# A hybrid decoder step on one core: gate-up weights by halves, dealt parts, idle products and an earlier pick

## The reference

```python
h = rms_norm(x, g_mix); z = h @ w_in              # 1024 -> 4096
... # pooling mixer, gated convolution, two merge gates, w_o
x = x + mixed @ w_o

xt = rms_norm(x, g_ffn)                            # 264 rows count
logits = xt @ w_router + b_router                  # 32 experts
top_val, top_idx = lax.top_k(logits, 4); gates = softmax(top_val)
# for each expert e, over the rows that picked it:
hgu = x_e @ w_gu[e] + b_gu[e]                      # 1024 -> 2048, 8 MiB of weights
gate = minimum(hgu[:, :1024], 7); up = clip(hgu[:, 1024:], -7, 7)
y_e = (gate * sigmoid(1.702 * gate) * (up + 1)) @ w_down[e] + b_down[e]   # 4 MiB
x = x + sum over the four experts of gate * y_e
y = rms_norm(x, g_final)
```

## Time and profile before

| | |
|---|---|
| median of 3 runs | 1090.71 us (1090.71 to 1091.31) |
| the profiled execution | 1091.32 us |
| its span | 1089.5 us |
| busy: PE, PEld, DVE, ACT, POOL | 1049.2, 510.2, 462.5, 174.2, 8.9 us |
| packets of DMA, bytes | 52479, 432.63 MB, mean 397 GB/s |
| granted clock of TensorE | 0.997 of full speed |

### The profile page before, as it was taken

How to read it: one execution, slowest core, us unless ns; L and a number is a source line. 1 busy time by engine, 2 the same in 40 slices (tenths; PEclk the granted TensorE clock), 3 DMA queues, 4 the chain that set the end, 5 groups by cost and what they waited for, 6 DMA issues and landing times.

```text
span 1089.5 us, 17315 instructions
## 1 busy us (share of the span) xinstructions
PE 1049.2 (96%) x7081; PEld 510.2 (47%) x7081; DVE 462.5 (42%) x780; ACT 174.2 (16%) x296; POOL 8.9 (1%) x21
## 2 busy tenths in 40 slices
PE   8999999999999999999999999999999999999995
PEld 7999975434433444434344333333444333333332
DVE  5577675333333333333333333333333333333344
ACT  5435533100000000000000000000000000000012
POOL 1000100000000000000000000000000000000000
PEclk9999999999999999999999999999999999999998
DMA  9872899999999999999999999999999999999994
GB/s 295 289 227 103 324 405 375 429 420 426 428 429 427 429 428 430 427 429 428 429 428 428 429 428 428 428 429 428 428 429 428 429 428 429 429 428 431 426 425 170
DMA packets 52479, 432.63 MB, mean 397 GB/s; under 512 B 4630, under 2 KB 21546, under 8 KB 26205
## 3 DMA queue, kind: packets, MB, share of 16 engines
q1 hardware_dynamic: 50959, 431.04, 95.3%
q10 hardware_dynamic: 1494, 1.22, 0.4%
HBM read 431.10 MB, written 1.39 MB: 397 GB/s over the span
## 4 chain that ended last, share of the span: by engine, by line
PE 65%; DMA 26%; DVE 4%; issue 4%; ACT 1%; SPq 1%; DVEq 0%; ACTq 0%
PE PS L1153 24%; PE PS L1182 17%; DMA down_ring<-in_w_down_dram 14%; DMA gu_ring<-in_w_gu_dram 11%; PE PS L918 9%; PE PS L1082 3%; PE PS L1122 2%; PE PS L949 2%; PE PS L1124 1%; PE PS L1196 1%; PE PS L1166 1%; PE PS L1164 1%; DVE pick_twice L1596 1%; PE PS L1200 1%; PE PS L869 0%
## 5 line engine op out<-in xcount | busy, mean ns | idle before, releaser
L1153 PE MATMUL PS<-gu_ring,XgT 128*64 128x512 f32 x2048 | 470.5, 599 | 6.7 <-DMA gu_ring<-in_w_gu_dram 6.7
L1153 PEld LDWEIGHTS PS<-gu_ring,XgT 128*64 128x64 f32 x2048 | 134.5, 136 | 272.0 <-issue 244.5
L1182 PE MATMUL PS<-down_ring,actT 128*64 128x512 f32 x984 | 219.3, 596 | 7.7 <-DMA down_ring<-in_w_down_dram 7.7
L1628 DVE TENSOR_TENSOR Y<-PS,Y 128x1024 f32<-128x1024 f32 (+1 forms) x96 | 117.0, 1220 | 253.7 <-PE PS L1124 253.7
L1182 PEld LDWEIGHTS PS<-down_ring,actT 128*64 128x64 f32 x984 | 67.5, 137 | 134.8 <-issue 119.3
L1666 DVE SCALAR_TENSOR_TENSOR y_low<-PS,slot_gate,y_high 128x512 fp32r<-128x512 f32 x31 | 23.3, 750 | 228.6 <-ACT y_high L804 228.6
L816 ACT ACTIVATE work<-PS 128x512 f32<-128x512 f32 x32 | 19.1, 597 | 454.8 <-PE PS L1153 454.8
L918 PE MATMUL PS<-h_high,win_high 128*128 128x264 f32 (+2 forms) x256 | 71.2, 287 | 0.0
L918 PE MATMUL PS<-h_high,win_low 128*128 128x264 f32 (+2 forms) x256 | 70.9, 286 | 0.0
L918 PE MATMUL PS<-h_low,win_high 128*128 128x264 f32 (+2 forms) x256 | 70.8, 285 | 0.0
L804 ACT ACTIVATE y_high<-PS,slot_gate 128x512 fp32r<-128x512 f32 x31 | 21.3, 687 | 258.9 <-PE PS L1182 258.9
(11 more groups left out here) (236 smaller groups left out, 778.2 us busy)
## 6 DMA issues: line engine op xcount, KB each, us to landing
gu_ring<-in_w_gu_dram SPq DMA_DIRECT2D x119, 2048.0 KB, 28.5
down_ring<-in_w_down_dram SPq DMA_DIRECT2D x60, 2048.0 KB, 21.2
gu_ring<-in_w_gu_dram SPq DMA_DIRECT2D x18, 1024.0 KB, 10.0
gu_ring<-in_w_in_dram SPq DMA_DIRECT2D x16, 1024.0 KB, 9.4
gu_ring<-in_w_down_dram SPq DMA_DIRECT2D x4, 1024.0 KB, 28.3
down_ring<-in_w_down_dram SPq DMA_DIRECT2D x3, 1024.0 KB, 9.4
down_ring<-in_w_pool_up_dram SPq DMA_DIRECT2D x1, 2048.0 KB, 11.6
gu_ring<-in_w_conv_out_dram SPq DMA_DIRECT2D x2, 1024.0 KB, 6.2
```

Source lines behind the costliest of these rows:

```text
L1153: last = mm(PS[SLOTS * h:SLOTS * h + SLOTS, b, :], XgT[:, k, :], w[:, D * b + HALF * h:D * b + HALF * h + HALF], start=(k == 0), stop=(k = ...
L1182: last = mm(PS[SLOTS * h:SLOTS * h + SLOTS, bank, :], acts[:, f % 4, f // 4, :], rows[:, f, HALF * h:HALF * h + HALF], start=(f == 0), sto ...
L1628: tt(Y[rows, t, :].rearrange("p (h n) -> p h n", h=2), PS[rows, bank:bank + 2, :], Y[rows, t, :].rearrange("p (h n) -> p h n", h=2), ALU.a ...
```

## The change

**Halves.** For items 4 to 29 and the second half of item 3, `load_half` loads 4 MiB at once: four k-steps, a partition reads four adjacent rows, a run of 32 KB. SP waits for four k-steps to be free, not two; PE waits before k-steps 0 and 4 only. Items 2, 3 (first half), 30 and 31 are still loaded by row or chunk, with semaphores of their own. The chunks now lie inside the halves' layout: a run of 16 KB out of every 32. The step between features that are dealt to one partition is four in place of two, everywhere.

**Dealt parts.** `part` and `keep_rest` read `Y` with a step of four and write the parts in the order in which the gather takes them, so its weights (`XP`) are contiguous.

**Idle products.** `fill_early` puts a product of 512 columns of ones at three places of the routing chain.

**Picks.** In `item` on DVE, `make_twice` stands ahead of `add_rows`.

```diff
-                by_r = gffn_rows.rearrange("m (p r) -> m r p", r=2)
-                for q in range(2):
+                by_r = gffn_rows.rearrange("m (p r) -> m r p", r=CH)
+                for q in range(CH):
...
+            def load_half(e, parity, h):
+                src = w_gu[0, bass.ds(e, 1), HALF * h:HALF * h + HALF, :].rearrange("a (p r) n -> (a p) (r n)", r=CH)
+                at = KT * parity + CH * h
+                sp.dma_start(gu_ring[:, at:at + CH, :].rearrange("p s n -> p (s n)"), src
+                             ).then_inc(half_landed[2 * parity + h], 16)
...
-            def item_gu(i, e, parity, chunks=range(CH)):
-                for m in chunks:
-                    sp.wait_ge(gu_used, 8 * i + (2 * m - 14))
-                    load_gu(e, parity, m)
+            def item_gu(i, e, parity, halves=range(2)):
+                for h in halves:
+                    sp.wait_ge(gu_used, 8 * i + (4 * h - 12))
+                    load_half(e, parity, h)
+
+            def item_chunk(i, e, parity, m, signal):
+                sp.wait_ge(gu_used, 8 * i + (2 * m - 14))
+                load_gu(e, parity, m, signal)
...
-            item_gu(2, 2, 0, (1, 2, 3))
-            item_gu(3, 3, 1)
+            for m, signal in ((1, half_landed[0]), (2, third_chunk), (3, half_landed[1])):
+                item_chunk(2, 2, 0, m, signal)
+            for m, signal in ((0, fourth_chunk), (1, half_landed[2])):
+                item_chunk(3, 3, 1, m, signal)
+            item_gu(3, 3, 1, (1,))
...
+            for u in range(2):
+                for m in range(CH):
+                    item_chunk(more * E + (E - 2 + u), E - 2 + u, u, m, gu_landed[CH * u + m])
+                item_down(more * E + (E - 3 + u), E - 3 + u)
...
-                nc.scalar.activation(dst, Y[rows, t, cols], ACT.Copy, scale=stat[rows, 3, t:t + 1]
+                nc.scalar.activation(by_fours(dst), dealt(Y[rows, t, cols]), ACT.Copy, scale=stat[rows, 3, t:t + 1]
...
             pe.wait_ge(pick_early, 1)
+            fill_early()
             pe.wait_ge(resid, 5)
             turn_rows(1, 1)
             turn_tails()
+            fill_early()
             pe.wait_ge(x2_kept, 5)
...
-                stt(rests[(t, h)][rows, :], Y[rows, t, cols], stat[rows, 3, t:t + 1], src, ALU.mult, ALU.subtract
-                    ).then_inc(first_rest, 1)
+                stt(by_fours(rests[(t, h)][rows, :]), dealt(Y[rows, t, cols]), stat[rows, 3, t:t + 1], by_fours(src),
+                    ALU.mult, ALU.subtract).then_inc(first_rest, 1)
...
                 if before is not None:
                     swiglu(before, e_before)
+                    make_twice(before)
                 if two_before is not None:
                     for t in range(NT):
                         add_rows(two_before, t)
-                if before is not None:
-                    make_twice(before)
```

## The result

The changed kernel takes 1095.84 us (median of 5 runs, 1094.54 to 1097.69) beside 1090.72 us before (5 runs, 1090.71 to 1092.03): a ratio of 1.0046, 95% interval 1.0033 to 1.0059. Run once more, in a later group, it gave 1.0047 (1.0034 to 1.0060). So it is slower by about 5 us. The profiled execution has a span of 1093.3 us (1095.14 with what lies around it), 3.8 us over the 1089.5 us before. In the new code the gate-up product is L1193 (before L1153), the down product L1222 (L1182), ACT's first parts L761 (L732), DVE's rests L1516 (L1477), the first gather from `Y` L1136 (L1101), the load of a half L440.

The account below looks back on a forecast made before the run. It took the DMA queue, never empty from about 190 us on, as the bound; +1.5 - 1.5 + 0 + 0.1 - 0.2 + 0.1 = 0.0 us left the median at 1090.7 us, range 1087.2 to 1094.6.

Parts of the forecast that it names:

- both costs together: Queue running dry before item 4 at 4.2 us plus costlier strided ACT and DVE reads: 1095.6 us, left outside the range.
- the gap: Queue of transfers before item 4's first half, requested at 227.60 us, 4.24 us later than before: +1.5 us, bound 4.2.
- Part 3: Twelve ACT and DVE instructions reading `Y` at 16 bytes, six in series before the first gate-up: 0, between 0 and +2.2 us.
- The case: Rival: the six strided ACT and DVE reads in series cost 0.37 us more each: 1092.9 us, chance 0.15.
- part 4: Three idle PE products in the routing chain, mostly within waits, win nothing as the clock is full: +0.1 us.
- Part 1: Halves in place of chunks: item 4's first request comes 4.24 us later, the queue runs dry: +1.5 us, between 0.5 and 4.2.
- the full price of 4.2 us: Rival: the queue runs dry for most engines from 223.4 to 227.6 us: 1093.4 us, slower, chance 0.2.
- no later half could starve the queue: After item 4, PE returns slots every 27.6 us, the queue takes 29.4, so the stock grows 1.8 us per item.
- The tail's last wait is the same: At the end, items 30 and 31 keep 2 MiB chunks, so the last wait for a load doesn't change.
- Part 2: Gate-up loads in runs of 32 KB move faster over 53 halves, 519 us of queue: -1.5 us, between 0 and -3.6.
- the row of 425 GB/s: Single-row loads in 8 KB runs, 167 to 175 us, moved 425 GB/s; possibly a little low, so the gain too large.
- Part 5: Picks made right behind the SwiGLU end PE's 0.3 us wait per item; only the last, in the tail, counts: -0.2 us.

Follow-up runs that it names:

- early_two: The changed kernel with everything up to item 1 back at a step of two and the parts in plain order: 1089.78 us, 0.9986 of the kernel before.
- chunk_four: `early_two` with the first half of item 4 loaded as two 2 MiB chunks: 1090.45 us, 0.9986 of the kernel before.
- both_ends: `late_halves` with items 28 and 29 loaded by chunks too: 1090.01 us, 0.9989 of the kernel before.
- picks_only: The kernel before with only the picks of the way back made ahead of the additions: 1090.57 us, 0.9989 of the kernel before.
- all_chunks: `early_two` with every gate-up load as four 2 MiB chunks in the new layout: 1091.59 us, 1.0002 of the kernel before.
- reads_only: The changed kernel with every gate-up load as 2 MiB chunks, strided reads kept: 1098.46 us, 1.0065 of the kernel before.
- no_idle: The changed kernel without the three idle products of the routing chain: 1095.69 us, 1.0037 of the kernel before.
- late_halves: `early_two` with items 2 to 7 loaded by 2 MiB chunks and halves only from item 8 on: 1089.11 us, 0.9981 of the kernel before.

## Why the prediction was wrong

It said 1090.7 us, between 1087.2 and 1094.6, and it was 1095.84. Slower had a third of the chance; the size was outside. The sum that the range left out, both costs together, is 1095.6 us and looks like a hit, but that is luck: it has the gap at 4.2 us, which cost 1.9, and neither the gather from `Y` nor the clock.

**The bound** was read rightly: the queue sets the time from 190 us on, and what delays item 0 comes back one for one. The first down product's 6.0 us of delay are seen at the end, with the gap's and less what the halves bring.

**Part 3 is the step that failed, and twice.** *First, the rows that I trusted.* I took zero for the strided reads of ACT and DVE, from the copies of `table` (32 elements, 190 against 180 ns), and kept the copy of `bias_gu` (0.37 us on 512 elements) as a bound. Measured: 0.5 us on ACT, 0.4 on DVE. The 16-byte step costs about 1 ns per element on ACT (505 ns / 512) and 0.8 on DVE. On 32 elements that would be 25 to 30 ns beside the 180 of the whole operation, and the `table` rows compared two different operations, so they could hardly show it. The nearest row was the one with the most elements, not the one with the nearest step. The rule of the Trainium skill that I had weighed against it (Advanced Engine Details and Errata, section SBUF Cachelines) was right. Four in series paid, 1.8 us; two were hidden beside the gather. The case was priced at 2.2 us and would have been about right for this half. *Second, an instruction that I left out.* The document before the prediction says that the step becomes four everywhere, and it names `by_row` among the places that read by that step. I priced the twelve instructions of ACT and DVE and the gather's weights in `XP`, and not the eight products that take their weights from `Y` itself and stand last before the first gate-up. They cost 1.84 us.

**The clock** was no rival at all. I wrote of part 4 that the clock was full, so that idle products win nothing, and did not ask what would bring it down. In the changed kernel it fell (0.50 between 180 and 182 us), 1.7 us in the profiled execution and 2.6 in another one (first gate-up in 16.44 us).

**Part 1** was right in mechanism, and near in size: taken +1.5, between 0.5 and 4.2; measured 1.9 us of moved data here and 2.0 in `early_two`. There the half is issued at 227.83 us and lands 12.2 us later, at 240.0; the forecast was 240.05. Its sign was badly chosen: a share under 0.9 and a dip of 2 us or more between 226 and 231 us was to mean the full price of 4.2 us. `early_two` has 0.72 and 258 GB/s from 226 to 232 us, a dip of 6 x (1 - 258/428) = 2.4 us, and lost half that price. What else was wrong in it is that no later half could starve the queue. `chunk_four` shows that the next halves do, once item 4 doesn't. "The tail's last wait is the same" was wrong as well, PE waits for no load after some 998 us, but it costs nothing (`both_ends`).

**Part 2** was mis-sized: taken 1.5 us, bound 3.6. It is 0.15 us for each item's 8 MiB, 26.5 times, 4.0 us. Of the 519 us that these loads take, that is 0.8%, where the prediction had 0.35 or 0.7%: the upper end of its argument nearly held. I took the lower end because I doubted the row of 425 GB/s.

**Part 4** +0.1: nothing measurable, as forecast. **Part 5**: that PE's 0.39 us per item buy nothing in the loop isn't contradicted: `picks_only` has 0.9989, but `all_chunks`, with the same picks, 1.0002.

The sum with measured terms, and with the forecast -0.2 for the picks in the tail, which no run parts from the rest: +1.8 (four dealt reads) + 1.84 (gather from `Y`) + 1.7 (clock) + 1.9 (gap) - 4.0 (runs) - 0.2 = +3.0 us, and 0.7 of chance ahead of it all: 3.7 us, where the two profiled spans differ by 3.8. The medians differ by 5.1 us. The profiled execution is one of the two with a mean clock of 0.996 (1094.54 and 1095.14 us); the three with 0.991 to 0.993 took 1095.84 to 1097.69. They have no profile. That they fell longer behind the gather, as the second profile did, or already in the routing chain, as in `reads_only` and `no_idle` (both 0.993 in their profiles), is likely and not shown.

## What to carry to other kernels

When a layout changes, list every instruction that reads through it, on every engine, the weight loads of PE among them, and mark those on the chain that starts the pipeline. A change that wins 0.5% of a saturated queue is worth 4 us here, and a few strided f32 reads in front of the queue's first request can cost more than that; keep the old step for what stands on that chain and switch behind it (`late_halves`, 0.9981). And for the price of an access pattern take the row with the most elements, since a short operation hides a per-element cost in its fixed time.

## What the runs showed of the hardware

- A read of f32 from SBUF with a step of 16 bytes costs ACT 1220 ns in place of 715 for 512 elements and DVE 1144 in place of 747; with a step of 8 bytes 752 and 744 ns.
- An f32 weight load of 128x128 takes 196 ns with a step of 8 bytes and 330 with 16. The bf16 weights of the gather, with a step of 8 bytes, cost 1.99 us for 56 products against 1.74 contiguous, and also 1.74 with a step of 4 bytes.
- The granted clock of PE can fall to its lower level behind weight loads that keep it busy all the time (PEld 2.00 of 2.00 us from 176 to 178 us, then 0.50), and not in every execution of the same kernel. It also fell without that: `no_idle` had 0.58 from 170 to 174 us, with PE busy for 3.52 of the 4 us. `picks_only`, which has no strided read at 16 bytes, had 0.61 there in its profiled execution, so the changed kernel made a fall frequent, it didn't invent it.
- Requests of 4 MiB in runs of 32 KB for 8 of an item's 12 MiB, in place of 2 MiB in runs of 16 KB, bring 29.37 us for 12.58 MB down to 29.22. Run and request were changed together. The packets stay whole.
- A gap of 9.0 us between two requests, where it was 4.75 and 4.24 with a request between them, cost 2.0 us of moved data in `early_two`. With 2 MiB requests up to item 7 it is gone (409 GB/s from 176 to 260 us, where `early_two` has 400).
